# A routed SwiGLU layer: the wide expert places in three passes on high and low parts, a ring of 16 units, pairs and turns reordered

## What is computed

```python
logits = (xt @ w_router).astype(float32) + b_router
top_v, top_i = lax.top_k(logits, 2)
gates = softmax(top_v)
out = 0
for e in range(8):
    out += combine[:, e:e+1] * ((silu(xt @ w_gate[e]) * (xt @ w_up[e])) @ w_down[e])
```

## Time and profile before

| | |
|---|---|
| three runs, median (lowest to highest) | 1410.12 us (1407.42 to 1413.28) |
| profiled execution | 1409.12 us, span 1407.3 us, granted TensorE clock 0.99 |
| TensorE busy | 1335.0 us, 95% |
| VectorE, ScalarE busy | 458.1 us and 265.8 us, 33% and 19% |
| HBM read | 421.20 MB, 300 GB/s over the span |
| first product of the routed layer's experts | 522.65 us |

### The profile page before, as it was taken

How to read it: one execution, slowest core, us unless ns; L and a number is a source line. 1 busy time by engine, 2 the same in 40 slices (tenths; PEclk the granted TensorE clock), 3 DMA queues, 4 the chain that set the end, 5 groups by cost and what they waited for, 6 DMA issues and landing times.

```text
span 1407.3 us, 18535 instructions
## 1 busy us (share of the span) xinstructions
PE 1335.0 (95%) x7760; PEld 747.7 (53%) x7760; DVE 458.1 (33%) x1023; ACT 265.8 (19%) x491; POOL 98.8 (7%) x115
## 2 busy tenths in 40 slices
PE   6989999999999999999997898799999999999996
PEld 5856599999784665454443233254445444333332
DVE  7898865555589650040100010000101000100002
ACT  2551444443254210000000000011000001101101
POOL 4430100000551000000000000000000000000000
PEclk9999999999999999999999999999999999999998
DMA  9433355537121249999999999999596999999993
GB/s 303 144 127 120 108 193 180 180 120 266 64 90 62 105 173 422 416 412 417 421 422 420 423 422 420 420 410 407 240 418 278 375 418 416 417 417 416 417 424 135
DMA packets 106253, 423.49 MB, mean 301 GB/s; under 512 B 21632, under 2 KB 23864, under 8 KB 97976
## 3 DMA queue, kind: packets, MB, share of 16 engines
q1 hardware_dynamic: 100984, 421.75, 75.1%
q10 hardware_dynamic: 5184, 0.52, 0.4%
HBM read 421.20 MB, written 1.05 MB: 300 GB/s over the span
## 4 chain that ended last, share of the span: by engine, by line
PE 76%; DMA 12%; DVE 8%; issue 1%; SPq 1%; ACT 1%; POOL 0%; DVEq 0%; ACTq 0%
PE psall L2435 14%; DMA m_ring<-in_moe_w_down_dram 9%; PE psall L2579 9%; PE psall L2469 8%; PE psall L2550 5%; PE psall L2134 4%; PE psall L2488 4%; PE psall L2450 4%; PE psall L2233 3%; PE psall L2350 3%; PE psall L2352 3%; PE psall L2351 3%; DMA m_ring<-in_moe_w_up_dram 2%; PE psall L2299 2%; PE psall L2590 2%; PE psall L2406 2%
## 5 line engine op out<-in xcount | busy, mean ns | idle before, releaser
L2469 PE MATMUL psall<-m_ring,xeT 128*64 128x448 f32 (+1 forms) x1280 | 201.1, 544 | 11.1 <-DMA m_ring<-in_moe_w_up_dram 6.0
L2435 PE MATMUL psall<-m_ring,xeT 128*128 128x448 f32 x512 | 195.8, 543 | 0.0
L2005 DVE TENSOR_TENSOR hid<-e_silu,psall 128x448 f32<-128x448 f32 x28 | 17.4, 621 | 448.4 <-PE psall L2435 251.4
L2435 PEld LDWEIGHTS psall<-m_ring,xeT 128*128 128x128 f32 x512 | 97.4, 192 | 93.3 <-issue 92.9
L2469 PEld LDWEIGHTS psall<-m_ring,xeT 128*64 128x64 f32 (+1 forms) x1280 | 68.2, 126 | 137.3 <-issue 103.1
L2579 PE MATMUL psall<-m_ring,hidT 128*128 128x512 f32 (+1 forms) x336 | 125.0, 597 | 3.1 <-DMA m_ring<-in_moe_w_down_dram 3.1
L2550 PE MATMUL psall<-m_ring,hidT 128*32 128x256 f32 (+1 forms) x784 | 107.1, 496 | 18.2 <-DMA m_ring<-in_moe_w_down_dram 18.2
L1675 DVE TENSOR_TENSOR w_lo<-ring,w_hi 128x1024 fp32r<-128x1024 f32 x66 | 80.4, 1224 | 67.8 <-ACT w_hi L1266 67.7
L2350 PE MATMUL psall<-hnT_hi,w_hi 128*128 128x256 f32 x352 | 99.7, 283 | 0.7 <-DVE hnT_lo L1813 0.7
L2352 PE MATMUL psall<-hnT_hi,w_lo 128*128 128x256 f32 x352 | 99.5, 283 | 0.0
L2351 PE MATMUL psall<-hnT_lo,w_hi 128*128 128x256 f32 x352 | 98.9, 281 | 0.0
(11 more groups left out here) (341 smaller groups left out, 1482.8 us busy)
## 6 DMA issues: line engine op xcount, KB each, us to landing
m_ring<-in_moe_w_gate_dram SPq DMA_DIRECT2D x128, 896.0 KB, 22.2
m_ring<-in_moe_w_up_dram SPq DMA_DIRECT2D x128, 896.0 KB, 20.4
m_ring<-in_moe_w_down_dram SPq DMA_DIRECT2D x64, 1792.0 KB, 22.8
ring<-in_w_in_dram SPq DMA_DIRECT2D x10, 2048.0 KB, 12.4
ring<-in_ffn_w_gate_dram SPq DMA_DIRECT2D x5, 2048.0 KB, 10.4
ring<-in_ffn_w_up_dram SPq DMA_DIRECT2D x5, 2048.0 KB, 7.7
ring<-in_ffn_w_down_dram SPq DMA_DIRECT2D x5, 2048.0 KB, 7.9
ring<-in_w_out_dram SPq DMA_DIRECT2D x4, 2048.0 KB, 8.0
```

What stands on the lines that cost most here:

```text
L2435: ins = M(m_bank(key)[:, 0:MH], x[:, i, 0:P], weights(kind, i, s), start=(i == 0), stop=(i == KT - 1))
L2469: ins = M(m_bank(key)[q:q + shape[0], 0:MH], x[:, i, 0:shape[0]], w[:, m * MW + s * MH:m * MW + (s + 1) * MH], start=(i == 0), stop=(i == ...
```

## The change

- `ITEMS` becomes "AEBECDDD": pairs 128 + 32, 160 + 32, 96 + 64, 64 + 64. The first pair's turns become (0, 0, 1, 0, 0, 1).
- The ring has 16 units instead of 18; several small buffers move to make room for `part_hi` (four high parts of up to 1024 columns) and `xe_hi`.
- The wide places' 128 tokens are computed in three passes. A chunk's weights are cut into 24 parts: 16 k tiles of 896 columns, and eight of the down (`ROWS`; row 3 in two halves). ScalarE copies each to `part_hi` (`high`), VectorE writes weight minus high back into the ring in place (`low`), both up to four parts ahead of TensorE. Tokens and transposed hidden values are split too (`tokens_high`, `tokens_low`, `hidden_low`).
- For B the 32-column products come first, in gate and up and in the down, since they read the whole weight; the subtraction of a part waits for them. Units are freed after two parts each.
- `second_tiles` moves from the third step of the first pair to that of the second. `scatter_rest` is dropped.

```diff
-MSLOT = 18
+MSLOT = 16
+AHEAD = 4
+ROWS = [(r, 0, 2) for r in range(3)] + [(3, 0, 1), (3, 1, 1)] + [(r, 0, 2) for r in range(4, MB)]
-ITEMS = "AEDDBECD"
+ITEMS = "AEBECDDD"
-TURNS[0] = (0, 1, 0, 0, 0, 1)
...
             for kind, who in (("g", "A"), ("u", "V")):
...
+                for i in range(KT):
+                    self.part((it, c, kind, i))
+                    if i < KT - 1:
+                        self.event(("p", it, c, kind, i))
+                    else:
+                        for q in range(2):
+                            self.add((kind, it, c, q), who, self.rolling())
+                    self.part_done.append(self.n)
+            order = [(kind, h) for kind in "gu" for h in range(UH)]
+            if 32 in shape:
+                order.sort(key=lambda a: a[1])
+            for kind, h in order:
+                self.load(it, c, kind, h, ("p", it, c, kind, UK * h + 1) if h < UH - 1 else (kind, it, c, 1))
+            return
...
+            def high(upto):
+                while highs[0] < upto:
+                    n = highs[0]
+                    unit_wait(act, *part_unit(n))
+                    if n >= AHEAD:
+                        act.wait_ge(m_ready, experts.part_done[n - AHEAD])
+                    nc.scalar.activation(part_hi[:, n % AHEAD, 0:part_cols(n)[1]], part_raw(n),
+                                         ACT.Copy).then_inc(part_high, 1)
+                    highs[0] += 1
...
+            def wide_silus(it, c, first):
+                high(first + AHEAD)
...
+                high(first + KT + AHEAD)
+                for s in range(2):
+                    m_arrived(act, ("g", it, c, s))
+                    nc.scalar.activation(e_silu[:, s, :], m_bank(("g", it, c, s))[:, 0:MH],
+                                         ACT.Silu).then_inc(m_drained["A"], 1)
...
+            def low(upto):
+                while lows[0] < upto:
+                    n = lows[0]
+                    it, c, kind, i = experts.parts[n]
+                    dve.wait_ge(part_high, n + 1)
+                    if 32 in experts.shape(it):
+                        if kind == "d":
+                            dve.wait_ge(m_ready, experts.free[("qd", it, c)])
...
+                    V.tensor_tensor(part_raw(n, True), part_raw(n),
+                                    part_hi[:, n % AHEAD, 0:part_cols(n)[1]].bitcast(F32),
+                                    ALU.subtract).then_inc(part_low, 1)
+                    lows[0] += 1
...
+            low(2)
             take_tokens(0)
+            tokens_low(0)
+            low(AHEAD)
             gates_of_tokens()
...
-            for p, pos, it, c in experts.steps:
+            for n, (p, pos, it, c) in enumerate(experts.steps):
+                first, mine, then, further = experts.first_part[2 * n:2 * n + 4]
+                if experts.wide(it):
+                    low(first + AHEAD)
+                    if 32 in experts.shape(it):
+                        quad_hidden(it, c)
+                    low(mine)
+                low(min(mine + AHEAD, then))
                 hidden(it, c)
+                low(then)
...
-                if pos == 2 and p == 0:
+                if pos == 2 and p == 1:
                     second_tiles()
...
+                if len(experts.shape(it)) > 1 and experts.wide(it):
+                    hidden_low(it, c)
+                low(min(then + AHEAD, further))
+                if experts.shape(it) == (P,):
+                    hidden_low(it, c)
...
+                        pe.wait_ge(part_low, n + 1)
...
-                            ins = M(m_bank(key)[:, 0:MH], x[:, i, 0:P], weights(kind, i, s), start=(i == 0),
-                                    stop=(i == KT - 1))
...
+                            M(y, xe_hi[:, i, :], hi, start=(i == 0), stop=False)
+                            M(y, xe_lo[:, i, 0:P], hi, start=False, stop=False)
+                            ins = M(y, xe_hi[:, i, :], lo[:, cols], start=False, stop=(i == KT - 1))
...
+            def wide_down(it, c):
...
+                for j, (r, half, count) in enumerate(ROWS):
+                    n = experts.part_no[(it, c, "d", j)]
+                    pe.wait_ge(part_low, n + 1)
...
+                        M(y, hidT_hi[:, r, 0:P], hi, start=(c == 0 and r == 0), stop=False)
+                        M(y, hidT_low[r // 4][:, r % 4, :], hi, start=False, stop=False)
+                        ins = M(y, hidT_hi[:, r, 0:P], lo[:, cols], start=False, stop=(last and r == MB - 1))
...
-            scatter_rest(NI // 2 - 1)
             down(*before)
```

More of the change, by code:

```diff
@@ L116, in __init__ @@
         self.down(*before)
-        for j in range(4):
-            self.add(("sc", NI // 2 - 1, j), "V", (3, 4, 0, 1)[j])
+        self.first_part += [len(self.parts)] * 2
+        self.scatter(NI // 2 - 1, range(4))
         self.base = self.n, dict(self.count), self.silus, len(self.units)
@@ L189, in turned @@
     def turned(self, it, c):
-        for j in range(len(self.r_pieces(it))):
-            self.add(("tr", it, c, j), "A", self.misc())
+        for j, piece in enumerate(self.r_pieces(it)):
+            split = self.wide(it) and not piece[0]
+            self.add(("tr", it, c, j), "V" if split else "A", self.misc())
+            if split:
+                self.quiet(("th", it, c, j))
     def lane(self, it):
@@ L237, in narrow, with wide, part @@
         return self.shape(it) in ((64,), (32,))
+    def wide(self, it):
+        return self.shape(it)[0] == P
+    def part(self, key):
+        self.part_no[key] = len(self.parts)
+        self.parts.append(key)
     def chunks(self, it):
@@ L332, in down @@
                     self.event(("dn", it, c, m))
+            return
+        if self.wide(it):
+            if 32 in self.shape(it):
+                self.event(("qd", it, c))
+            for j in range(len(ROWS)):
+                self.part((it, c, "d", j))
+                if keys and j == len(ROWS) - 1:
+                    for key in keys:
+                        self.add(key, "A", key[2])
+                else:
+                    self.event(("dp", it, c, j))
+                self.part_done.append(self.n)
+            self.load(it, c, "d", 0, ("dp", it, c, 3))
+            self.load(it, c, "d", 1, keys[-1] if keys else ("dp", it, c, len(ROWS) - 1))
             return
@@ L547, in trunk_kernel @@
         fac = sb("fac", [P, 24, PAIRS])
+        fac_at = nc.sbuf_base - 4 * 24 * PAIRS
         w_if = sb("w_if", [P, KT, F_ROW + NH])
@@ L844, in unit_wait, with part_cols, part_raw, part_unit @@
                 eng.wait_ge(more_full[s], later(16 * n, 16 * experts.per_units[s], k))
+        def part_cols(n):
+            it, c, kind, i = experts.parts[n]
+            if kind == "d":
+                r, half, wide = ROWS[i]
+                return r * DM + 512 * half, 512 * wide
+            return i * MW, MW
+        def part_raw(n, low=False):
+            it, c, kind, i = experts.parts[n]
+            a, w = part_cols(n)
+            size = UNIT * (DOWN if kind == "d" else 1)
+            first, slots, _, _ = experts.slot[(it, c, kind, a // size)]
+            if low:
+                return ring_low[first, slots][:, a % size:a % size + w]
+            return m_ring[:, first:first + slots, :].rearrange("p s n -> p (s n)")[:, a % size:a % size + w]
+        def part_unit(n):
+            it, c, kind, i = experts.parts[n]
+            return it, c, kind, part_cols(n)[0] // (UNIT * (DOWN if kind == "d" else 1))
+        def xe_count(it, j):
+            return sum(len(experts.k_pieces(i)) for i in range(0, it, 2) if experts.wide(i)) + j + 1
         def v3(ap, k):
@@ L1340, in hidden_out @@
                     m_arrived(act, key, k)
+                    if experts.wide(it) and not base:
+                        nc.scalar.activation(hidT_hi[:, r0:r1, 0:P], v3(m_bank(key)[:, 0:(r1 - r0) * rows], r1 - r0),
+                                             ACT.Copy).then_inc(a_silu, 1)
+                        continue
                     nc.scalar.activation(hidT[:, r0:r1, base:base + rows],
@@ L1380, in _ @@
                     picks_out(p)
+                if pos == FIRST_DONE[p] - 1 and p + 1 < NI // 2 and experts.wide(2 * p + 2):
+                    tokens_high(2 * p + 2)
                 hidden_out(it, c)
```

171 lines of the change are left out of this document (128 added, 43 removed).

## The result

The changed kernel takes 1423.25 us (median of four runs, 1422.73 to 1423.70); the kernel before took 1410.55 beside it (four runs, 1407.42 to 1413.28). The ratio is 1.0097, with a 95% interval of 1.008 to 1.0115: slower by 12.7 us by the medians and 13.7 by the ratio, where 4.5 were forecast. The profiled execution's span is 1420.7 us, 13.4 more than before.

The account below looks back on a forecast made before the run. The DMA stream of expert weights was taken as the bound: 841 us for 384 units, plus idle DMA and the tail. Terms 8 + 1 + 0 - 4.5 = +4.5 us gave 1415 us, range 1402 to 1426 (chance 0.52).

Parts of the forecast that it names:

- Head and first pair: From 502 us: early loads fill the ring, then DMA stands still 18 to 19 us in 530 to 588; +8 us.
- The 160 pair: Pair 160 + 32: TensorE needs 249 us, 10 covered by the ring, 29 to 30 of idle DMA; +1 us.
- The ring: In the 160 pair: 16 units instead of 18 give 4.4 us less cover.
- Silu and copy: Start of up in a wide chunk: TensorE waits 1.1 us for gate's silu, behind one more high copy on ScalarE.
- Second_tiles: Narrow step of the 160 pair: its 16.5 us ahead of the subtractions make TensorE wait 9 us, bounds 5 and 13.
- Pass pitch: Wide products: one 448-column pass follows another after 0.20 us, bounds 0.19 and 0.21; three take 0.60 against 0.76 plain.
- Conversions and the DMA rate: Copies and subtractions at the ring: their effect on the DMA rate was left open, and nothing was added for it.
- The tail: Behind the last weights: 12.5 us from the last byte to the last scatter, instead of 17; -4.5 us.
- The signs: Trace marks named ahead, among them DMA share near 0.68 in 530 to 588 and 28 to 32 us idle in pair two.
- Units freed early enough: Faster rival: freeing in twos and late units hiding `second_tiles` take up to 29 us off, 1384 to 1403; chance 0.27.
- Conversions set the pace: Slower rival: 192 parts through two in-order queues slow six wide chunks by 22 us, 1424 to 1450; chance 0.16.
- Passes bring nothing: Rival: a 448-column pass takes 0.25 us, so gate and up gain nothing, 20 us slower, 1435; chance 0.05.

Follow-up runs that it names:

- e11_hold: Changed kernel, but only eight of the 16 units of expert 0 loaded before the ranks are known: 1424.53 us, 1.0093.
- e4_turns: Changed kernel with the first pair's turns put back to wide, narrow, wide, wide, wide, narrow: 1416.55 us, 1.0048.
- e2_order: Kernel before, plain products, with the new order of pairs, first-pair turns wide, wide, narrow, a 16-unit ring and no early scatter: 1419.94 us, 1.0084.
- e12_plain: Kernel of e2_order with the first pair's turns wide, narrow, wide, wide, wide, narrow: 1416.57 us, 1.0051.
- e6_warm: Changed kernel with ten more 128x448 products in TensorE's 8.2 us wait behind `second_tiles`, third wide chunk of the 160 pair: 1422.24 us, 1.0099.
- e5_ring16: Kernel before with only the ring cut from 18 to 16 units: 1418.69 us, 1.0061.
- e8_silu: Changed kernel with the high copy of the fourth part of up issued behind the silus of gate instead of ahead: 1415.05 us, 1.0034.
- e1_tiles: Changed kernel with `second_tiles` moved from the narrow step of the 160 pair to that of the third pair: 1415.34 us, 1.0044.
- e7_light: Changed kernel with each subtraction cut to 64 columns, which the third pass reads over and over: 1417.11 us, 1.0049.
- e3_passes: Changed kernel with the old order of pairs, old first-pair turns and `second_tiles` in the first pair's third step: 1415.39 us, 1.004.

## Why the prediction was right or wrong

The time lies within the range, near its upper end, but the forecast was no change that can be measured, +4.5 us, and it is slower by 12.7. That 1402 to 1426 holds it is owed in part to the range's width, since one step was off by more than the whole forecast. In the trace the parts make +13.7, so 9.2 are missing: 2.7 in the first pair, 7.0 in the 160 pair, and 0.5 the other way in the tail.

*Head and first pair, +8 forecast, +10.7 in the trace.* The mechanism was right: a ring filled early with the wide expert stands full behind its slow chunks. Idle DMA in 530 to 588 is 58 x (1 - 274/419) = 20.1 us against 18 to 19. The "5 units more at 530" that the step started from are no gain in themselves, as e11_hold shows: what is loaded by 588 us follows from what TensorE has freed. The turns make the loss: putting them back wins 6.9 us with the passes (e4_turns) and 4.7 with plain products (e2_order to e12_plain).

*The 160 pair, +1 forecast, +8.0 in the trace.* This step failed. I put TensorE's work at 249 us, and it is 258. The loss of cover was right: before, 253.9 - 210 = 44 us too slow and 32.7 lost, 11 covered; now 48 and 40.7, 7 covered, 4 less for two units of ring. The levels were not: I read 15 us of cover and 29 of idle DMA from the share, which reads high where single transfers start again; the bytes give 11 and 32.7. By stretches between the starts of each kind of work, in us:

| | forecast | changed | plain, same order (e2_order) |
|---|---|---|---|
| 128-token gate and up | 81.2 | 85.7 | 97.0 |
| 32-column gate and up | 24.9 | 26.7 | 24.5 |
| wait behind `second_tiles` | 9 | 8.2 | 0 |
| wide downs with their 32 columns and waits | 59.3 | 66.0 | 62.7 |
| narrow gate, up and downs | 36.9 | 39.8 | 37.5 |
| transposes | 18 | 15.7 | 12.5 |
| gathers, scatters, picks | 16.7 | 15.9 | 16.4 |
| late units | 3 | (in the rows above) | (in the rows above) |
| sum | 249 | 258.1 | 250.7 |

Three terms were mis-sized. A chunk's gate and up is 20.9 us and not 20.3: the pitch is 0.204, and twice the second pass starts 0.3 us behind the first. The 42 passes of a down take 10.1 us and not 9.5 (pitch 0.232), and the downs have, beside the 1.4 us wait for the first part, one of 0.9 behind each narrow step and 2.1 for a late unit. (The 32-column row has a stand of 1.8 us in the first chunk, which the trace puts down to no engine.) And nothing was booked for the clock: in four places of the pair the granted clock falls for some microseconds, where before it does in two; plain products in the new order have none (1.00 in 720 to 980 us, above). Here are those of before, and then three of the changed kernel (the fourth is the one of e6_warm):

```profile
946.00:952.00 6.00, 6.00 (x42) 4.61 (x40) 1.66 (x3) 1.07 (x2) 0.00 (x0) 0.78 0.99 377
964.00:970.00 6.00, 5.14 (x17) 3.15 (x17) 0.00 (x0) 2.10 (x5) 0.00 (x0) 0.72 1.01 428
754.00:760.00 6.00, 6.00 (x59) 4.22 (x62) 0.42 (x1) 1.79 (x2) 0.00 (x0) 0.73 1.03 406
820.00:826.00 6.00, 5.43 (x39) 2.28 (x43) 1.00 (x2) 0.77 (x2) 0.00 (x0) 0.72 0.29 88
964.00:970.00 6.00, 4.03 (x35) 1.98 (x36) 1.96 (x2) 0.17 (x1) 0.00 (x0) 0.72 1.02 407
```

Each follows gathers, transposes or a short wait. A narrow gate and up takes 13.7 us with such a fall and 12.1 without, a narrow down 7.9 and 6.2, the third wide chunk 2.1 more than the others, the last down about 1.6: 7.1 us together, against some 3 before. Those 3 lie in the wide gate and up and the narrow downs, two rows which I had replaced by terms at full clock, so all of the 7.1 us are missing from my 249. With the other terms that were too low they make more than the missing 9; transposes, gathers and the wait behind `second_tiles`, 3.9 too high together, and the 3 for late units, which here stand in other rows, take the rest back. That filling a wait keeps the clock up was shown in one place, and 1.4 us were won there; how much of the 7.1 us could be had back was not tried.

The last column holds what I should have seen: by the forecast's own numbers the passes take 98.8 - 81.2 = 17.6 us off gate and up, yet the new order, with plain products, has the pair at 250.7 already; against that the passes give 11.3 us and take back 19.2: 8.2 for `second_tiles`, 3.3 in the downs, 3.2 in the transposes, 2.2 and 2.3 in the 32-column and narrow products (the falls of the clock are in these rows).

*The ring.* I booked the two units as 4.4 us less cover in the 160 pair, and that is what they cost there. By e5_ring16 they cost 8.6 us in the old order, half of it at the end of the first pair, where I had no term. That is as dear as any wait that the other runs took away.

*Silu and copy.* The wait at the start of up was found ahead, 1.1 us against 0.92 to 1.06 in seven places (and 2.3 in the first chunk). It was priced rightly and looked small, and in eight places it was as dear as any other wait: taking it out brings 8.9 us (e8_silu), against 7.5 for `second_tiles`, which the runs can't tell apart.

*Second_tiles.* 9 us forecast, 8.15 in the trace, 7.5 in time (e1_tiles). *Fifth part of the first chunk:* 4.3 forecast, 3.6 in the trace. *Downs:* 1.4 and 1.42. *Pass pitch:* 0.20 and 0.20. The plain product is 0.38 x 2 us in the rows, so three passes are 0.8 of it. The Trainium skill (FP8 and Floating Point Precision, TensorE Precision Notes) counts four passes for plain fp32; if each cost what a float32r pass costs, the ratio would be 0.75. The trace has 0.76/0.204, that is 3.7 of these passes, in a plain product, and so sides with the rows; the count of four is neither shown nor refuted by it.

*Conversions and the DMA rate.* What two more engines at the ring do to the rate was left open. The changed kernel moves 416 GB/s in 600 to 775 us beside 98.5 us of VectorE and 84.0 of ScalarE; e7_light, with the subtractions nearly gone, has 414 there, and 419 in its last full window as the changed kernel has. This agrees with the Trainium skill (SBUF — State Buffer, SBUF: two separate sides), by which engine and DMA ports can't contend.

*The tail, -4.5 forecast, -5.0 in the trace.* Behind the last byte 12.2 us, 12.5 forecast.

*The signs.* Most came as named. In 530 to 588 the share reads 0.76 where I had named 0.68, but the bytes are 274/419 = 0.65 of the full rate. The idle DMA of the second pair, 28 to 32 us as named, came to 40.7: the sign by which the failed step could be seen.

*The rivals.* Units freed early enough: no, e1_tiles shows that nothing covered `second_tiles`, and the pair lost more than before. Conversions set the pace: no, by e7_light and by the passes that stay 0.20 us apart in the changed kernel; but its sign and most of its size came true by another way, the places without cover. Passes bring nothing: true of the whole (e4_turns beside e12_plain), though not by its mechanism, since the pitch is 0.20 us. That a saving on TensorE can be eaten by the waits which it needs was in none of my cases; there, and in the clock, lay most of what was missing in the 160 pair.

## What to carry to other kernels

Cost a faster instruction together with every hand-over that it adds, and add both up in the same table, stretch by stretch, also for the version without it: here, in one pair, 11 us of TensorE were won and 19 given back, in pieces of 1 to 8 us. Where a ring is full, what TensorE waits comes off the end time, and waits in different places add up (7.5 + 6.9 + 8.9 gave 23.4), so the small ones that come eight times are worth as much as the one that is seen first. Price the ring's units too: two of 18 cost 8.6 us. An in-order helper queue should hold, ahead of a hand-over that the bottleneck engine waits for, nothing that could as well come behind it; two such moves, the old turns and one earlier hand-over turned a change that cost 13.7 us (ratio 1.0097) into one that brings 14.7 (0.9896).

## What the runs showed of the hardware

The granted clock of TensorE falls to 0.5 (1.2 GHz) in a wait of 8.2 us and stays there for about 4 us of work behind it; it did not fall when that wait was filled with plain products (e6_warm). In these traces it also falls for a few microseconds after stretches of gathers and transposes and waits of 0.7 to 2.1 us (to 0.72 to 0.78 over 6 us in the pair of 160, and to 0.50 in one place of e1_tiles). The profiled executions of kernels with the passes ran at a mean of 0.978 to 0.985, those with plain products at 0.988 to 0.994. In the twelve runs of e3_passes the clock and the time went together, from 0.982 and 1407.5 us to 0.971 and 1422.5 us (correlation -0.81); which of the two is cause, and why one program's runs differ so, stays open.

Two subtractions of different width, 896 and 64 columns, took 1.09 and 0.23 us on VectorE, while the DMA engines moved 416 and 419 GB/s beside the first and 414 and 419 beside the second.
